# Two transformer blocks on one core: the second mixer's projections and output product put among its attention, and the softmax shift's diagonal written in one operation

## What is computed

```python
def second_block(x, ...):
    h = rms_norm(x, norm_mix_pre)
    qa, ka, va, qb, kb, vb = jnp.split(h @ w_in, SPLITS, axis=-1)
    qa = apply_rope(rms_norm(qa, q_norm_a), ang_axial)   # 8 heads of 64
    ka = apply_rope(rms_norm(ka, k_norm_a), ang_axial)   # 2 heads
    out_a = global_attention(qa, ka, va)                 # softmax over all 512 keys
    qb, kb = apply_rope(qb, ang_1d), apply_rope(kb, ang_1d)
    out_b = window_attention(qb, kb, vb, sink_b)         # |distance| <= 128, and a sink
    mixed = concat([rms_norm(out_a, group_norm_a), rms_norm(out_b, group_norm_b)]) @ w_out
    x = x + rms_norm(mixed, norm_mix_post)
    h = rms_norm(x, norm_ffn_pre)
    f = (silu(h @ w_gate) * (h @ w_up)) @ w_down
    return x + rms_norm(f, norm_ffn_post)
```

## Time and profile before

| | us |
|---|---|
| median of 3 runs | 2176.59 (2175.07 to 2177.75) |
| profiled run, its own time | 2175.67 |
| its span | 2173.6 |
| PE, DVE, ACT, POOL busy | 2004.6, 1105.3, 505.0, 1226.0 |
| first panel of the second mixer begins | 1447.4 |
| first scores of its attention | 1545 |
| last values of its attention end | 1700.3 |
| last tile of w_out is joined | 1755.5 |

### The profile page before, as it was taken

One profiled execution on the slowest core, in us unless ns is written; L12 is line 12 of the kernel. 1 busy time (PEld: TensorE's weight loads), 2 busy tenths in 40 slices (PEclk: granted clock), 3 DMA queues, 4 the chain that ended last, 5 costly groups with the idle time before them and its releaser, 6 DMA issues.

```text
span 2173.6 us, 25282 instructions
## 1 busy us (share of the span) xinstructions
PE 2004.6 (92%) x8955; PEld 1623.3 (75%) x8955; DVE 1105.3 (51%) x1308; ACT 505.0 (23%) x916; POOL 1226.0 (56%) x752
## 2 busy tenths in 40 slices
PE   7999999789989899889999999998888869999996
PEld 5888888467767687678778888876676748888884
DVE  5333430557676467666653332039778684333104
ACT  3111100344334342350111110022365321111001
POOL 4666666336645545436666666664445456666661
PEclk9999999889999999999999999999999979999998
DMA  4333323212211223102323333233100113333220
GB/s 150 97 97 96 97 96 88 78 49 78 68 49 50 59 59 87 49 1 83 92 88 96 96 96 98 96 90 84 49 0 1 39 49 97 96 96 96 97 87 39
DMA packets 259808, 163.83 MB, mean 75 GB/s; under 512 B 30380, under 2 KB 249582, under 8 KB 259614
## 3 DMA queue, kind: packets, MB, share of 16 engines
q1 hardware_dynamic: 258080, 157.90, 24.8%
q10 hardware_dynamic: 1662, 5.06, 0.7%
HBM read 160.81 MB, written 2.13 MB: 75 GB/s over the span
## 4 chain that ended last, share of the span: by engine, by line
PE 77%; DVE 14%; ACT 3%; issue 2%; POOL 2%; ACTq 1%; DMA 0%; POOLq 0%; DVEq 0%; SPq 0%
PE bank L710 12%; PE bank L711 12%; PE bank L712 12%; PE bank L778 5%; PE bank L777 5%; PE bank L779 5%; PE bank L971 3%; PE bank L972 3%; PE bank L973 3%; DVE work L1978 2%; PE bank L841 2%; DVE work L1917 1%; PE bank L1176 1%; PE bank L1177 1%; PE bank L1178 1%
## 5 line engine op out<-in xcount | busy, mean ns | idle before, releaser
L597 POOL TENSOR_TENSOR w_lo<-raw,w_hi 128x1024 fp32r<-128x1024 f32 x298 | 746.1, 2504 | 24.9
L595 POOL TENSOR_SCALAR w_hi<-raw 128x1024 fp32r<-128x1024 f32 x298 | 320.5, 1075 | 711.9 <-PE bank L712 340.9
L710 PE MATMUL bank<-u_hi,w_hi 128*128 128x512 f32 x1184 | 476.3, 402 | 28.8 <-DVE u_lo L1866 19.1
L711 PE MATMUL bank<-u_lo,w_hi 128*128 128x512 f32 x1184 | 465.4, 393 | 0.0
L712 PE MATMUL bank<-u_hi,w_lo 128*128 128x512 f32 x1184 | 465.0, 393 | 0.0
L710 PEld LDWEIGHTS bank<-u_hi,w_hi 128*128 128x128 f32 x1184 | 224.6, 190 | 91.3 <-issue 25.5
L711 PEld LDWEIGHTS bank<-u_lo,w_hi 128*128 128x128 f32 x1184 | 225.0, 190 | 49.5 <-issue 4.7
L712 PEld LDWEIGHTS bank<-u_hi,w_lo 128*128 128x128 f32 x1184 | 224.9, 190 | 47.1
L1892 DVE TENSOR_TENSOR work<-bank,work 128x512 f32<-128x512 f32 x66 | 45.6, 691 | 285.1 <-PE bank L712 285.1
L779 PE MATMUL bank<-hid_hi,w_lo 128*128 (+1 forms) x480 | 186.9, 389 | 0.0
L778 PE MATMUL bank<-hid_lo,w_hi 128*128 (+1 forms) x480 | 186.9, 389 | 0.0
(11 more groups left out here) (463 smaller groups left out, 3293.7 us busy)
## 6 DMA issues: line engine op xcount, KB each, us to landing
raw<-in_w_in SPq DMA_DIRECT2D x52, 512.0 KB, 3.7
raw<-in_ffn_w_gate SPq DMA_DIRECT2D x44, 512.0 KB, 3.8
raw<-in_ffn_w_up SPq DMA_DIRECT2D x44, 512.0 KB, 3.7
raw<-in_ffn_w_down SPq DMA_DIRECT2D x44, 512.0 KB, 3.5
raw<-in_w_gate SPq DMA_DIRECT2D x22, 512.0 KB, 3.7
raw<-in_w_up SPq DMA_DIRECT2D x22, 512.0 KB, 3.7
raw<-in_w_down SPq DMA_DIRECT2D x22, 512.0 KB, 3.7
raw<-in_w_branch SPq DMA_DIRECT2D x12, 512.0 KB, 3.4
```

The source lines that it names most:

```text
L595: pool.tensor_scalar(w_hi[:, s, :], raw[:, k, :], 1.0, 1.0, ALU.mult, ALU.mult).then_inc(hi_done, 1)
L597: pool.tensor_tensor(w_lo[:, s, :], raw[:, k, :], w_hi[:, s, :].bitcast(F32), ALU.subtract).then_inc(split_ready, 1)
L710: pe.matmul(outs[:, 0:n], wh, rhs_hi[:, c, :], start=(c == 0), stop=False)
L711: pe.matmul(outs[:, 0:n], wh, rhs_lo[:, c, :], start=False, stop=False)
```

## The change

Six of the twelve panels of the second mixer (ka, qa0, va, qa1, kb, qa2) stay ahead of the attention. The other six (B2_AHEAD is 6) and the half of w_out that belongs to group A become fillers, 48 and 32 chunks of three matmuls, which PE takes one by one between the parts of a step: five in a head. The attention does the eight heads of A first and then the eight of B. Scores have one bank instead of two and stand in the second and third step of a head, transposed scores two banks instead of three; the diagonal is written in the fourth step. All rotations, sums of squares and the B values share bank AUX one after another, and norms and rotations of qa1 to qa3, kb and all of qb are done by DVE within the attention (`later`, by step number). POOL splits ten units between its subtractions, each where PE has used up one. The low part of the probabilities has three small tiles. w_out is laid out as eight units of two output tiles and one group; `half_out` scales the A half of a tile out of PSUM within the attention, `join` adds the B half after it. In every attention of the kernel the diagonal is one tensor_tensor of the identity and the maxima, both repeated by their access patterns.

```diff
+B2_PANELS = "ka", "qa0", "va", "qa1", "kb", "qa2", "qa3", "qb0", "qb1", "vb", "qb2", "qb3"
+B2_BANK = dict(zip(B2_PANELS, (2, 3, 4, 5, 4, 5, 4, 5, 4, 5, 4, 5)))
+B2_AHEAD = 6
...
+        b2_ph = at("b2_ph", [P, TT * S], b2a, F32R)
+        b2a += 8192
+        prob_lo = at("prob_lo", [P, 3, S], work_at + 7 * 2048, F32R)
+        for st in (ast, bst):
+            st |= {"ph": b2_ph, "pl": None, "off": SPREAD}
...
         b2_heads = []
         for j in range(4):
             for job in pair(ast, whole, q=qa2[j]):
-                b2_heads.append(job | {"q_ready": S_B2 + (LAST_A if j == 3 else 2 * j + 3) + 1, "v_ready": S_B2 + V_A + 1})
+                b2_heads.append(job | {"q_ready": s_no(f"qa{j}") + 1, "v_ready": s_no("va") + 1})
+        for j in range(4):
             for job in pair(bst, window, q=qb2[j], extra=lambda *a, j=j: band(qb2[j][0], *a), extra_t=band_t, sinks=j):
-                b2_heads.append(job | {"q_ready": S_B2 + (LAST_B if j == 3 else 2 * j + 2) + 1, "v_ready": S_B2 + V_B + 1})
+                b2_heads.append(job | {"q_ready": s_no(f"qb{j}") + 1, "v_ready": s_no("vb") + 1})
...
+        B2_BANKS = (0,), (2, 3), (6, 7), None
+        FIRST_FILL = 4
+
+        A_HALF = [(m, c) for m in range(2) for c in range(3)] + [(0, 3), (1, 3)]
+        A_HALF += [(m, c) for m in range(2, KC) for c in range(4)]
+
+        def fill_step(k):
+
+            head, i = (k - FIRST_FILL) // 5, (0, 1, 1, 2, 2)[(k - FIRST_FILL) % 5]
+            return (4 * head if head < 8 else 32 + 5 * (head - 8)) + i
...
-            for u in range(U_B2, U_WO2 + SPL):
+            for u in range(U_B2, U_B2 + B2_AHEAD + SPL):
                 one(u)
-            low_parts(A_B2, b2_heads)
-            for u in range(U_WO2 + SPL, U_GU3 + SPL):
+            emptied = {fill_step(KC * k + KC - 1): U_B2 + B2_AHEAD + k for k in range(10)}
+            for x, step in enumerate(b2_steps):
+                if step[2] is not None:
+                    low_part(A_B2, b2_heads, step)
+                if x in emptied:
+                    one(emptied[x] + SPL)
+            for u in range(U_WO2 + 4 + SPL, U_GU3 + SPL):
...
+                hooks = {
+                    2: lambda: (pe.wait_ge(h_std, H_B2 + 4), turn_a(2)),
+                    3: lambda: aux_free("a2", lambda: turn_b(0)),
+                    5: lambda: aux_free("b0", lambda: turn_a(3)),
+                    9: lambda: aux_free("a3", lambda: sum_a(4, AUX)),
+                    13: lambda: turn_a(4),
+                    17: lambda: aux_free("a4", lambda: turn_b(1)),
+                    20: lambda: aux_free("b1", lambda: turn_b(2)),
+                    27: values_b,
+                    32: lambda: (pe.wait_ge(s_lo, s_no("vb") + 1), turn_b(3)),
+                    40: group_sum_a,
+                    44: lambda: (pe.wait_ge(g_std, 1), turn_b(4)),
+                }
+                for x, (h, i, kb, t, b) in enumerate(b2_steps):
+                    if x in hooks:
+                        hooks[x]()
+                    scores_t(h, i, kb, t)
+                    more = h + 1 < len(b2_heads) and i in (1, 2)
+                    if i <= 2:
+                        go_on(fill, 1)
+                    if more:
+                        scores(h + 1, 2 * i - 2)
+                    if x >= PV_LAG and b2_steps[x - PV_LAG][2] is not None:
+                        h_, i_, kb_, t_, b_ = b2_steps[x - PV_LAG]
+                        values_mm(h_, i_, kb_, b_)
+                    if i in (1, 2):
+                        go_on(fill, 1)
+                    if more:
+                        scores(h + 1, 2 * i - 1)
...
-                    for qt in range(TT):
-                        last = dve.tensor_scalar(shift[:, h % 2, qt * P:(qt + 1) * P], ident, neg[:, h % 2, qt:qt + 1],
-                                                 None, ALU.mult)
-                    last.then_inc(a_shift, 1)
+                    dve.tensor_tensor(shift[:, h % 2, :].rearrange("p (i n) -> p i n", i=TT),
+                                      ident.unsqueeze(1).to_broadcast([P, TT, P]),
+                                      neg[:, h % 2, :].unsqueeze(2).to_broadcast([P, TT, P]), ALU.mult).then_inc(a_shift, 1)
...
+                def half_out(m):
+                    if m % 2:
+                        dve.wait_ge(unit_done, U_WO2 + m // 2 + 1)
                     else:
...
+                        dve.wait_ge(g_half, m // 2 + 1)
+                    dve.tensor_tensor(mo[:, m, :], bank[Q_BANK + m % 2][:], W[0], ALU.mult).then_inc(g_part, 1)
...
+                later = {
+                    0: [lambda: norm_a(2)],
+                    2: [lambda: turn_a(2)],
+                    3: [lambda: (low_a(2), dve.wait_ge(tab_scaled, 1), turn_b(0))],
+                    4: [lambda: norm_a(3)],
+                    6: [lambda: (low_b(0), turn_a(3), raw_a_of(4))],
+                    8: [lambda: low_a(3)],
+                    12: [lambda: norm_a(4)],
+                    14: [lambda: turn_a(4)],
+                    16: [lambda: low_a(4)],
+                    17: [lambda: turn_b(1)],
+                    18: [lambda: low_b(1)],
+                    20: [lambda: turn_b(2)],
+                    22: [lambda: low_b(2)],
+                    25: [lambda: raw_v_of(1)],
+                    28: [lambda: value_low(s_no("vb"), bst, AUX)],
+                    33: [lambda: turn_b(3)],
+                    36: [lambda: low_b(3)],
+                    41: [lambda: factor(0)],
+                    45: [lambda: turn_b(4)],
+                    47: [lambda: low_b(4)],
+                }
+                for m in range(KC):
+                    x = fill_step(KC * (len(B2_PANELS) - B2_AHEAD) + A_HALF.index((m, 3))) + 1
+                    first.setdefault(max(42, x), []).append(lambda m=m: half_out(m))
...
+                for x in range(len(b2_steps) + PV_LAG + 3):
+                    h, i = b2_steps[x][:2] if x < len(b2_steps) else (len(b2_heads), 0)
+                    for step in first.get(x, []):
+                        step()
+                    if h + 1 < len(b2_heads) and i in (1, 2):
+                        maxes(h + 1, 2 * i - 2)
+                        maxes(h + 1, 2 * i - 1)
+                    if h + 1 < len(b2_heads) and i == 3:
+                        diagonal(h + 1)
+                    if x - PV_LAG - 2 in b2_ends:
+                        output(b2_ends.index(x - PV_LAG - 2))
...
             def join(m):
-                b = 2 * (m % 3)
-                dve.wait_ge(unit_done, U_WO2 + m + 1)
-                dve.tensor_tensor(mo[:, m, :], bank[b][:], W[2], ALU.mult).then_inc(g_part, 1)
+                b = (4, 5, 0, 1, 2, 3, 4, 5)[m]
+                if m % 2:
+                    dve.wait_ge(unit_done, U_WO2 + 4 + m // 2 + 1)
+                else:
+                    dve.wait_ge(g_half, 4 + m // 2 + 1)
                 if m >= 2:
                     dve.wait_ge(res, KC + m - 1)
-                dve.tensor_tensor(W[4 + m % 2], bank[b + 1][:], W[3], ALU.mult).then_inc(g_part, 1)
-                dve.wait_ge(g_part, 2 * m + 2)
+                dve.tensor_tensor(W[4 + m % 2], bank[b][:], W[1], ALU.mult).then_inc(g_part, 1)
+                dve.wait_ge(g_part, KC + m + 1)
                 dve.tensor_tensor(mo[:, m, :], mo[:, m, :], W[4 + m % 2], ALU.add).then_inc(res, 1)
-            norm_recip(N_GRP, groups=2)
-            dve.wait_ge(n_rec, N_GRP + 2)
```

540 lines of the change are left out of this document (321 added, 219 removed).

## The result

The changed kernel takes **2223.2 us** (median of 4 runs, 2222.2 to 2223.9); the kernel before, on the same chip, 2177.1 (4 runs). The ratio is 1.0213 with a 95% interval of 1.0195 to 1.0231: 46 us slower. The prediction was 2189, slower by 12, with a range of 2160 to 2206. The sign is right, the size is not. The profiled execution has a span of 2221.2 us (before: 2173.6).

What follows compares the result with a forecast made beforehand. Neither TensorE nor VectorE alone was the bound: two queues wait in turns, and the order of small DVE steps decides. Second mixer +14.5 us, less 2 for the diagonal elsewhere: +12.5, so 2189 us, range 2160 to 2206.

Steps and rivals of the forecast that it cites:

- Part 1: Second mixer up to the first scores: attention starts 41 us earlier, at about 1504; gain about 2 us.
- Part 2: Second mixer's attention: 182 us of PE work plus 47 us of waits (41 to 57), ending at 1733.
- step 3: Group A, four steps a head: rotation b0 waits for a2, whose bank it shares; 3.0 to 3.6 us.
- step 5: Group A: rotation a3 waits for its norm, behind diagonal, split and rotation; 2.7 to 3.6 us.
- step 8: Group A: two splits, rotation, copy and diagonal on DVE make PE wait 3.4 to 4.5 us.
- step 13: Group A: diagonal, two reciprocals and two products behind the maximum make PE wait 5.9 to 6.4 us.
- step 16: Group A: rotation, group split and diagonal on DVE make PE wait 2.1 to 3.1 us.
- steps 1, 18, 21 and 24: Remaining waits listed for the first six heads of group A, 4.4 to 6 us together.
- rival with the clock: Attention: six to eight longer waits lower PE's clock, losing 8 to 15 us more; 2198 to 2210, chance 0.10.
- faster rival: Attention: fillers hide DVE's chains, waits w under 30 us; about 2153, or 2166 with half the waits; chance 0.23.
- no change: Attention: waits of 30 to 39 us instead of 47 give 2172 to 2181; chance 0.14.
- Part 3: Tail after the attention, DVE's opening and eight joins: 34 to 40 us, taken 37, ending at 1770.

Runs made afterwards that it cites:

- early: The changed kernel with the next head's scores, maxima and diagonal one step earlier, as before the change; 2201.5 us.
- early_turns: The changed kernel with scores, maxima and diagonal one step earlier and three of PE's rotations one step later; 2190.6 us.
- one_bank: The kernel before, its second mixer with one score bank instead of two, two transposed-score banks instead of three, second score behind the values; 2193.9 us.
- busy_all: The changed kernel with 228 matmuls of zeros in PE's queue ahead of its long waits for diagonals and rotations; 2206.9 us.
- warm: The kernel before with the one-operation diagonal and 140 matmuls of zeros at five places where PE waits long; 2163.0 us.

## Why the prediction was right or wrong

In the prediction's own terms, for the profiled execution: it put the first score at 1502 (1504 less 2), measured 1500.5, -1.5; the attention at 229 us, measured 266.4, +37.4; the tail at 37, measured 35.3, -1.7; behind it +0.9. Sum +35.1, which is 2221.2 against the forecast span of 2186.1. So one term carries the miss, and within it one part: of the +37.4 the waits are 6.2, the work 2 and the clock, which the sum had at nothing, 29.3.

- **Part 1, right.** 57.4 us from the start of the window to the first score, forecast 56.6; from PE's first matmul of the panel it is 51.7, forecast 50.9.
- **Part 2, work, right.** 182 forecast, 184 measured, or 187.5 with the low clock counted beside work only.
- **Part 2, waits, right in sum, partly by luck.** 47 forecast, 41 to 57; measured 53.2. By place, forecast and measured: step 3: 3.0 to 3.6, 4.3; step 5: 2.7 to 3.6, 5.8; step 8: 3.4 to 4.5, 3.4; step 13: 5.9 to 6.4, 6.1; step 16: 2.1 to 3.1, 4.4; steps 1, 18, 21 and 24: 4.4 to 6, all other waits of group A 2.4; group A and heads 6 and 7 in all 22 to 28, 29.4 with 2.9 at head 6. Step 5 was probably undersized because step 3's rotation had itself been late, which I had not carried forward.
- **Group B, right in sum only.** 19 to 27 forecast, 23.9 measured, but not from the terms named. The three heads behind an output: 14 to 17, 11.9 (3.8, 4.4, 3.8); my own terms add up to 6.6 to 7.1 us, not to 6.9 or more, and less the 2.3 they are 4.3 to 4.8 each. The square root of group A: 3.3, measured 1.7 (the exponential behind its two table loads, at 1680.3), and no filler waited for half_out. POOL's splits, rotations and the rest: 2 to 6, measured 10.3. The largest piece of that is a wait that I had not foreseen:

```profile
1665.27 0.62 ACT L1430 ACTIVATE raw_x<-bank 128x512 f32<-128x512 f32 x1
1665.99 0.77 PE L1237 MATMUL bank<-oua_hi,w_hi 128*128 128x512 f32 x1 [3.45 <-issue]
```

  The profile names no releaser. By the order of the program this filler, the first for the second output tile, waits for ScalarE's copy of the last query panel out of the same bank, and it starts 0.1 us after that copy ended. The copy stood behind group A's last output on ScalarE's queue, and that one behind the diagonal of 2.88 us and a reciprocal.
- **The cause in group B, true but no lever.** The output stood ahead of the diagonal as described, and moving it behind gave 1.2 us. I had followed the chain to the next wait and not to the one after. The rows above show this for one of the three.
- **The clock, the step that failed.** My sum was waits plus work at full clock. The rival with the clock allowed 8 to 15 us for six to eight longer waits and a chance of 0.10. Measured: 29.3 us in the attention, 24.6 more than before. I had priced it by the 4.6 us of a stretch whose waits for DVE were at most 1.5 us, and not by what follows a longer wait: behind ten of the eleven longest waits the granted clock was 0.50 to 0.76 for the next 2 us, and at half in all for 3 to 6 us behind most of them (behind the eleventh, 2.9 us at 1622, it was 1.00); the earlier trace rows had shown one such place. With 13 to 16 us given back by keeping PE busy, the clock alone explains at least a good third of the 35 us between forecast and result; the rest of its 24.6 cannot be told apart from the waits that it lengthens, since a PE at half clock also delays the scores that DVE waits for.
- **The faster rival, and no change:** they needed waits under 39 us. Even the best order tried, with 29 us of waits, has 14 of clock. The form of that rival's sum holds once w is waits and clock together: 2176.6 + 82.5 - 34.5 = 2224.6 for the changed kernel, 2201 for early, 2185 for early_turns (measured 2223.2, 2201.5, 2190.6). That is the steady work of the table said once more, and no proof of a cause.
- **The diagonal, direction right, size too small.** Price of the operation as forecast in group A (0.7 to 0.9; 0.74 in the mean), above it in group B (1.03, the longest 2.88). Forecast 2 us outside the second mixer, bounds 0 to 4, from PE's waits for the diagonal, 0.3 us. The largest single gain was behind another name: a wait for ScalarE's square some links down the chain. All in all the diagonal is worth 8 to 10 us. The 0.51 us that I had estimated for the four short operations came from a table row of the Trainium skill, "VectorE: DVE Perf Modes", section ⚠️ The TRN2 errata — SBUF-src ops pay a fixed extra latency per instruction, which the same section says under-predicts single operations; the trace has 0.88 us.
- **Part 3, right.** Tail 34 to 40 forecast, 35.3 measured, PE idle 11.9 us ahead of the post norm's sum (10 to 15). The opening took 14.8 us (1767.0 to 1781.8), as forecast, the eight joins 20.4 (17.6 to 25), although their addition alone took 1.15 us in the mean and not the 2.2 that I had used. The last reciprocal and the first join:

```profile
1778.40 3.35 DVE L2581 RECIPROCAL work<-work 128x512 f32<-128x512 f32 x1 [2.64 <-ACT work L1944]
1781.79 0.69 DVE L2646 TENSOR_TENSOR work<-bank,work 128x512 f32<-128x512 f32 x1
```

What stays open: what made the rest of the 35 us beyond the 13 to 16 of the clock, and how the change would do with two score banks. One bank costs 16 us in the old order; that it costs as much in the new one is argued from the 16.7 us of waits for maxima in early_turns, and was not tried.

## What to carry to other kernels

Price a wait of TensorE twice: its own length, and the stretch at half clock behind it. In this kernel the second was about half as much again as the waits themselves (0.4 to 0.7 of them in the kernels of the table without zeros, 0.2 in the one before), and about half of it came back in length when PE was kept busy. In one_bank such stretches stood behind waits of 2.3 us. Before filling a queue with panels, ask which of the waits they stand behind; and when an operation is moved out of one chain, follow it through every engine's queue, since its time can come out at the next one. The diagonal was cheaper as one long instruction than as four short ones beside a busy GpSimd, and its gain showed in waits that bear another name.

## What the runs showed of the hardware

- Matmuls of zeros on an idle TensorE made the program faster: 16.3 us in the changed kernel, 5 to 6 in the other, with the granted clock of the stretch rising from 0.89 to 0.97 and from 0.69 to 1.00 (busy_all, warm).
- With no wait over 2.6 us, 175 us of attention had a granted clock of 0.90 (one_bank; 0.97 before): half clock for 3.1 to 6.8 us behind each of five waits of 2.3 to 2.6 us, none behind three of 1.6.
- Four operations of 128 columns lasted 3.77 us beside POOL's (the third 2.41), one of 512 columns 0.73 in the same place, and 2.88 where POOL's had started first.
